# Attention of the second block by pairs of heads, with probabilities normalised before the transposes and output by features

## The chip, the cores and the metric

The kernel runs on one core of a Trainium2 chip. The metric is the device time of one execution in microseconds. A core has a matrix engine (PE, TensorE), VectorE (DVE), ScalarE (ACT), GpSimd (POOL) and SyncE (SP). Each works through its own list of instructions in order and waits for the others on counting signals (semaphores).

## What is computed

Two blocks in fp32, each of two layers, follow one another over 256 tokens of width 1024. The change lies in the second block, whose layers hold an FFN, a mixer and an FFN. In the mixer are two attentions (branch a, with a bias table over a neighbourhood, and branch b, with a window of 128 and a sink), each of six heads of 64, and a convolution:

```
def second_block(...):
    for l in range(DEPTH):
        ...
        ya = neighborhood_attention(qa, ka, va, ka_c, va_c, na_rpb[l], rows)
        yb = window_attention(qb, kb, vb, kb_c, vb_c, sw_sink[l])
        yc = conformer_conv(ux, conv_dw_w[l], conv_dw_b[l], conv_ln_g[l], conv_ln_b[l])
        x = x + mx[5] * merge_branches(ya, yb, yc, gx, b_gate[l], w_out_a[l], w_out_b[l], w_out_c[l], w_out[l])
        if not last:
            ya_c = context_attention(qa_c, ka_c, va_c, None)
            yb_c = context_attention(qb_c, kb_c, vb_c, sw_sink[l])
```

Queries are cut in tiles of 128. Tiles 0 and 1 are the tokens, which look at 256 own and 256 context keys (512); tiles 2 and 3 are the context, which looks at its own 256 keys and is there in layer 0 only. Branch b has two heads of keys and values for six heads of queries.

## The kernel before

**Order.** `plan()` writes one list of names for all engines: D is half a step of dense matmul, V an eviction, H and S the high and the low part of a weight (a cast on ACT and a subtraction on DVE), B a step of the second block's attention, C a tap of the convolution on DVE (two instructions), P a rotation, N a norm. Each engine has a generator for each name, and the list says in which order its parts stand on every engine. In the mixer the steps B are spread evenly between D, C and P by `mix()`: eight D with half of the first branch's, eight D with the rest and four C, then a stretch without D (B, four P and nine C), and then 24 D with all of the second branch's and 18 C. A D over 512 tokens is 12 matmuls of 512 columns, or nine or six in the products with the attention's output.

**Dense work.** Each weight is split in a high and a low fp32r part and each product takes three matmuls (`dense()`). Dense results go to the banks PS0 to PS2, and PS3 where four tiles are needed.

**Attention (`attention2` of the tensor, scalar and vector programs).** A job is a head of one query tile. In step i PE does the scores of job i (in PS4 or PS5 by turns), the transposes of the probabilities of job i - 1 (in PS6) and the product of job i - 2 with the values (in PS7). DVE adds the bias or the mask, takes the negated maximum, in branch b limits it by the sink, and then does the reciprocal of the sum of job i - 1 and scales the output of job i - 2 into O2. ACT does the exponential with its sum, in branch b the sink's too, and copies the transposed probabilities to PT2. After six heads, three transposes turn a tile of O2 into features, and ACT and DVE split it into YH2 and YL2. PE's transposes wait for the exponential alone:

```
                            q.wait_ge(*ab.at("exp", l, g))
                            if g:
                                q.wait_ge(*ab.at("pt", l, g - 1))
                            for x in range(2 if jobs[j][1] >= 2 else 4):
                                y = e.transpose(PS[6][:, 128 * x:128 * x + 128], P2[:, g % NB, 128 * x:128 * x + 128], IDN)
```

The wait for ACT's exponential of job i - 1 is met long before, since a D lies between two steps nearly everywhere.

Of the kernel before, what the change touches and what calls it, by code (L numbers as in the profile page):

```python
# [3 lines left out]
DEPTH = 2  # L4
# [50 lines left out]
def plan():  # L55
# [106 lines left out]
    def mixer(l, last, norm):  # L162
# [19 lines left out]
        nb = 6 * nq // 128 + 2  # L182
# [120 lines left out]
def program(nc, t, out):  # L303
# [81 lines left out]
    P2 = at("P2", 112.5, [128, 2, 512])  # L385
    PT2 = at("PT2", 116.5, [128, 2, 512])
    O2 = at("O2", 120.5, [128, 2, 384])
    ST2 = at("ST2", 123.5, [128, 256])
    TM2 = at("TM2", 124.5, [128, 3, 512])
# [58 lines left out]
    def jobs2(l):  # L448

        nt = 2 if l == DEPTH - 1 else 4  # L450
        return [[(br, q, h) for q in range(nt) for h in range(6)] for br in range(2)]


    def tensor_program(e):
# [17 lines left out]
        def operand(un, k, halves):  # L472
# [21 lines left out]
            if un.buf == "Y2":  # L494
                nt = 2 if l == DEPTH - 1 else 4
                if kk < 6:
                    q.wait_ge(*vb.at("y", l, kk // 3, nt - 1))
# [235 lines left out]
        def attention2():  # L733
            LAG, NB = 1, 2
            for l in range(DEPTH):
                nt = 2 if l == DEPTH - 1 else 4
                for br, jobs in enumerate(jobs2(l)):
                    n = len(jobs)
                    g0 = br * n
                    for i in range(n + 2 * LAG):  # L740
                        if i < n:
                            _, x, h = jobs[i]
                            g = g0 + i
                            if g < 2:
                                q.wait_ge(*vn.at("h", 4 + 3 * l, 7, 0))
                            else:
                                q.wait_ge(*ab.at("exp", l, g - 2))
                            k0, nk = (256, 256) if x >= 2 else (0, 512)
                            if br == 0:
                                hs, Q_, K_ = h % 2, QA[:, h // 2, :], QA[:, 3 + h // 2, :]  # L750
                                q.wait_ge(*ad.at("qa", l, h // 2))
                                q.wait_ge(*ad.at("qa", l, 3 + h // 2))
                            else:
                                hs, Q_, K_ = h // 3, QB[:, h % 3, :], QB[:, 3, :]
                                q.wait_ge(*vp.at("ro", l, h % 3))
                                q.wait_ge(*vp.at("ro", l, 3))
                            mm(PS[4 + g % 2][:, 0:nk], half(Q_, hs)[:, 128 * x:128 * x + 128],
                               half(K_, hs)[:, k0:k0 + nk]).then_inc(*pb.inc("s", l, g))
                        j = i - LAG
                        if 0 <= j < n:  # L760
                            g = g0 + j
                            q.wait_ge(*ab.at("exp", l, g))
                            if g:
                                q.wait_ge(*ab.at("pt", l, g - 1))
                            for x in range(2 if jobs[j][1] >= 2 else 4):
                                y = e.transpose(PS[6][:, 128 * x:128 * x + 128], P2[:, g % NB, 128 * x:128 * x + 128], IDN)  # L766
                            y.then_inc(*pb.inc("t", l, g))
                        j = i - 2 * LAG
                        if 0 <= j < n:
                            _, x, h = jobs[j]  # L770
                            g = g0 + j
                            vcol = 64 * h if br == 0 else 384 + 64 * (h // 3)
                            P = PS[7][:, 64 * (g % 4):64 * (g % 4) + 64]
                            q.wait_ge(*ab.at("pt", l, g))
                            if g:
                                q.wait_ge(*vb.at("o", l, g - 1))
                            k0, kt = (2, 2) if x >= 2 else (0, 4)
# [3 lines left out]
                            z.then_inc(*pb.inc("v", l, g))  # L781
                            if h == 5:
                                q.wait_ge(*vb.at("o", l, g))
                                if br or x:
                                    q.wait_ge(*vb.at("y", l, *((br, x - 1) if x else (0, nt - 1))))
                                else:
                                    q.wait_ge(*ad.at("v2", l, 3))
                                for y in range(3):
                                    z = e.transpose(PS[3][:, 128 * y:128 * y + 128],
                                                    O2[:, (nt * br + x) % 2, 128 * y:128 * y + 128], IDN)  # L790
                                z.then_inc(*pb.inc("y", l, br, x))
                        yield
# [11 lines left out]
        def lnorm():  # L804
            for l in range(DEPTH):
                nt = 2 if l == DEPTH - 1 else 4
                for x in range(nt):
                    P = PS[4]
                    q.wait_ge(*ab.at("exp", l, 12 * nt - 1))
# [22 lines left out]
    def scalar_program(e):  # L832
# [232 lines left out]
        def attention2():  # L1065
            LAG, NB = 1, 2
            for l in range(DEPTH):
                nt = 2 if l == DEPTH - 1 else 4
                for br, jobs in enumerate(jobs2(l)):
                    n = len(jobs)  # L1070
                    g0 = br * n
                    for i in range(n + 2 * LAG):
                        if i < n:
                            _, x, h = jobs[i]
                            g = g0 + i
                            nk = 256 if x >= 2 else 512
                            q.wait_ge(*vb.at("m", l, g))
                            if g >= NB:
                                q.wait_ge(*pb.at("t", l, g - NB))
                            af(P2[:, g % NB, 0:nk], PS[4 + g % 2][:, 0:nk], ACT.Exp, bias=ST2[:, g:g + 1],  # L1080
                               acc=ST2[:, 64 + g:65 + g]).then_inc(*ab.inc("exp", l, g))
                            if br:
                                af(ST2[:, 192 + i:193 + i], vec("sink", 6 * l + h), ACT.Exp, bias=ST2[:, g:g + 1]).then_inc(
                                    *ab.inc("sink", l, g))
                        j = i - LAG
                        if 0 <= j < n:
                            g = g0 + j
                            nk = 256 if jobs[j][1] >= 2 else 512
                            q.wait_ge(*pb.at("t", l, g))
                            if g >= NB:  # L1090
                                q.wait_ge(*pb.at("v", l, g - NB))
                            af(PT2[:, g % NB, 0:nk], PS[6][:, 0:nk], ACT.Copy).then_inc(*ab.inc("pt", l, g))
                        j = i - 2 * LAG
                        if 0 <= j < n and jobs[j][2] == 5:
                            x = jobs[j][1]
                            q.wait_ge(*pb.at("y", l, br, x))
                            af(YH2[:, 3 * br:3 * br + 3, 128 * x:128 * x + 128],
                               PS[3][:, 0:384].rearrange("p (i n) -> p i n", n=128), ACT.Copy).then_inc(*ab.inc("yh", l, br, x))
                        yield
# [27 lines left out]
    def vector_program(e):  # L1127
# [402 lines left out]
        def attention2():  # L1530
            LAG = 1
            for l in range(DEPTH):
                nt = 2 if l == DEPTH - 1 else 4
                for br, jobs in enumerate(jobs2(l)):
                    n = len(jobs)
                    g0 = br * n
                    for i in range(n + 2 * LAG):
                        if i < n:
                            _, x, h = jobs[i]
                            g = g0 + i  # L1540
                            nk = 256 if x >= 2 else 512
                            P, M = PS[4 + g % 2], ST2[:, g:g + 1]
                            q.wait_ge(*pb.at("s", l, g))
                            if x < 2 and br == 0:
                                q.wait_ge(*vk.at("bm", l))
                                tt(P[:, 0:256], P[:, 0:256], BM[:, x, h, :], ALU.add).then_inc(*vb.inc("b", l, g))
                                q.wait_ge(*vb.at("b", l, g))
                            elif x < 2:
# [424 lines left out]
```

## Time and profile before

| what | us |
|---|---|
| median of three runs | 2559.02 (2554.39 to 2559.24) |
| the profiled execution | 2551.03 |
| its span | 2549.2 |
| PE matmul busy | 2409.1 (95%) |
| DVE busy | 1576.8 (62%) |
| ACT busy | 874.9 (34%) |
| mean granted TensorE clock | 0.967 of full |

The profiled execution is 8 us below the median of the three timed runs, so differences are formed against its own 2551.03 and then put on the median. Busy shares are unions of instruction times. PE's instructions are pipelined, so what a matmul costs is read from one start to the next, not from its duration. An fp32 matmul stands in the trace as two instructions.

### The profile page before, as it was taken

How to read it: one execution, taken by the hardware profiler on the slowest of the kernel's cores; microseconds unless marked ns; L12 is line 12 of the kernel's file. 1: busy time of each engine (PE TensorE's matmuls, PEld its weight loads, DVE VectorE, ACT ScalarE, POOL GpSimd, SP SyncE). 2: the span in 40 equal slices, each digit the busy share in tenths (PEclk: the TensorE clock that was granted, in tenths of full speed). 3: DMA queues.
4: the chain of work that ended last, by engine and by line, in shares of the span. 5: the costliest groups of instructions: out<-in, count | busy, mean ns of one | idle time of the engine just before them, and what ended most of it. 6: DMA issues, size and time to landing. Idle time of an engine off the chain costs nothing.

```text
span 2549.2 us, 33154 instructions
## 1 busy us (share of the span) xinstructions
PE 2409.1 (95%) x13210; PEld 2028.7 (80%) x13210; DVE 1576.8 (62%) x2950; ACT 874.9 (34%) x1488; POOL 238.4 (9%) x321
## 2 busy tenths in 40 slices
PE   4898897899999999999999999999999999999998
PEld 4788776788888866678888888888888887788998
DVE  4886886576766446664469976654343345766655
ACT  3344344322222333433332222232222233444443
POOL 1010011100001200002211111100000030012001
PEclk9998998899999997999999999999999999999999
DMA  6543542254453310112336665522322232144553
GB/s 234 178 142 117 171 157 78 101 184 161 166 173 124 116 48 23 46 61 93 105 116 216 220 215 198 190 81 93 99 91 93 98 116 79 58 133 158 185 183 125
DMA packets 95354, 333.00 MB, mean 131 GB/s; under 512 B 11040, under 2 KB 13216, under 8 KB 94816
## 3 DMA queue, kind: packets, MB, share of 16 engines
q1 hardware_dynamic: 70496, 244.41, 28.7%
q0 software_dynamic: 23376, 84.80, 10.4%
q8 instruction: 105, 1.72, 0.3%
q10 hardware_dynamic: 1328, 1.66, 0.2%
q14 instruction: 49, 0.40, 0.1%
HBM read 329.78 MB, written 2.48 MB: 130 GB/s over the span
## 4 chain that ended last, share of the span: by engine, by line
PE 83%; DVE 10%; issue 3%; ACT 3%; POOL 1%; DMA 1%; ACTq 0%; POOLq 0%; DVEq 0%
PE PS L458 81%; DVE WL L1131 2%; PE PS L766 1%; ACT WH L840 1%; DVE NT L1140 1%; DVE HL L1140 1%; DVE JK L1141 1%; DVE AR L1141 1%; DVE PJ L1140 1%; DVE ST L1144 0%; DMA CST<-in_cst 0%; DVE CV L1140 0%; POOL SS L1722 0%; ACT HH L840 0%; DVE O L1135 0%
## 5 line engine op out<-in xcount | busy, mean ns | idle before, releaser
L840 ACT ACTIVATE WH<-RAW 128x1024 fp32r<-128x1024 f32 (+2 forms) x482 | 494.4, 1026 | 1061.1 <-PE PS L458 1060.8
L458 PE MATMUL PS<-HH,WH 128*128 128x512 f32 (+1 forms) x2136 | 763.7, 358 | 13.2 <-DVE HL L1140 5.9
L458 PE MATMUL PS<-HH,WL 128*128 128x512 f32 (+1 forms) x2136 | 751.7, 352 | 0.0
L458 PE MATMUL PS<-HL,WH 128*128 128x512 f32 (+1 forms) x2136 | 751.5, 352 | 0.0
L1131 DVE TENSOR_TENSOR WL<-RAW,WH 128x1024 fp32r<-128x1024 f32 (+2 forms) x482 | 572.1, 1187 | 171.7 <-ACT WH L840 170.6
L458 PEld LDWEIGHTS PS<-HH,WH 128*128 128x128 f32 x2136 | 407.9, 191 | 81.4 <-issue 9.2
L458 PEld LDWEIGHTS PS<-HH,WL 128*128 128x128 f32 x2136 | 408.0, 191 | 57.5
L458 PEld LDWEIGHTS PS<-HL,WH 128*128 128x128 f32 x2136 | 408.7, 191 | 55.6
L458 PE MATMUL PS<-GH,WH 128*128 128x512 f32 (+1 forms) x776 | 271.0, 349 | 0.0
L458 PE MATMUL PS<-GH,WL 128*128 128x512 f32 (+1 forms) x776 | 270.2, 348 | 0.0
L458 PE MATMUL PS<-GL,WH 128*128 128x512 f32 (+1 forms) x776 | 270.2, 348 | 0.0
L1140 DVE SCALAR_TENSOR_TENSOR FT<-FT,PS 128x512 f32<-128x512 f32 (+1 forms) x185 | 110.4, 597 | 252.0 <-ACT FT L840 184.0
L1141 DVE SCALAR_TENSOR_TENSOR AR<-AR,CB 128x1024 f32<-128x1024 f32 x144 | 178.0, 1236 | 2.4 <-DMA AR<-in_w_adaT 2.4
L1140 DVE SCALAR_TENSOR_TENSOR X<-PS,MOD,X 128x256 f32<-128x256 f32 x192 | 86.5, 480 | 140.5 <-PE PS L458 140.2
L458 PEld LDWEIGHTS PS<-GH,WH 128*128 128x128 f32 x776 | 146.0, 188 | 21.0 <-DVE GL L1131 0.2
L458 PEld LDWEIGHTS PS<-GL,WH 128*128 128x128 f32 x776 | 146.0, 188 | 20.7
L458 PEld LDWEIGHTS PS<-GH,WL 128*128 128x128 f32 x776 | 146.0, 188 | 20.6
L1801 POOL DMA_DIRECT2D AR<-in_w_adaT x144 | 77.0, 535 | 811.9 <-DVE AR L1141 691.6
L841 ACT ACTIVATE P<-PS,ST 128x512 f32<-128x512 f32 (+2 forms) x104 | 57.9, 557 | 235.2 <-DVE ST L1144 142.6
L1141 DVE SCALAR_TENSOR_TENSOR JK<-AR,CB 128x1024 bf16<-128x1024 f32 x112 | 137.5, 1228 | 1.4 <-DMA AR<-in_w_adaT 1.4
L458 PE MATMUL PS<-H1H,WH 128*128 128x256 f32 x384 | 117.6, 306 | 16.6 <-DVE WL L1131 15.0
L1722 POOL TENSOR_TENSOR SS<-SS,SQ 128x256 f32<-128x256 f32 (+1 forms) x59 | 65.9, 1117 | 706.0 <-ACT SQ L840 703.7
(219 smaller groups left out, 3045.5 us busy)
## 6 DMA issues: line engine op xcount, KB each, us to landing
RAW<-in_wst SPq DMA_DIRECT2D x420, 512.0 KB, 3.5
AR<-in_w_adaT POOLq DMA_DIRECT2D x144, 512.0 KB, 3.8
RAW<-in_wst SPq DMA_DIRECT2D x48, 384.0 KB, 3.0
BM<-rpb_rows POOLq DMA_DIRECT2D x48, 64.0 KB, 2.9
CB<-in_cc POOLq DMA_DIRECT2D x2, 1024.0 KB, 9.2
RAW<-in_wst SPq DMA_DIRECT2D x8, 256.0 KB, 2.7
RAW<-in_wst SPq DMA_DIRECT2D x4, 396.0 KB, 5.2
rpb_rows<-in_rpb POOLq DMA_DIRECT2D x2, 697.5 KB, 9.9
```

What stands on the lines that cost most here:

```text
L458: return e.matmul(o, l, r, start=start, stop=stop)
L766: y = e.transpose(PS[6][:, 128 * x:128 * x + 128], P2[:, g % NB, 128 * x:128 * x + 128], IDN)
L840: return e.activation(o, i, f, bias=bias, scale=scale)
L841: return e.activation(o, i, f, bias=bias, scale=scale, accum_out=acc)
L1131: return e.tensor_tensor(out=o, in0=a, in1=b, op=op)
L1140: return e.scalar_tensor_tensor(out=o, in0=a, scalar=s, in1=b, op0=op0, op1=op1)
L1141: return e.scalar_tensor_tensor(out=o, in0=a, scalar=s, in1=b, op0=op0, op1=op1, accum_out=acc)
L1722: return e.tensor_tensor(out=o, in0=a, in1=b, op=op)
L1801: e.dma_start(AR[:, y % 2, :], t["w_adaT"][l, x, :, :]).then_inc(adw[y % 2], 16)
```

## The change

A job becomes a pair of heads of one query tile: heads 2p and 2p + 1 in branch a, p and p + 3 in branch b, which lie in partitions 0 to 63 and 64 to 127 of one tile of Q and K. There are half as many jobs and `nb` follows: 14 steps for 26 in layer 0, eight for 14 in layer 1. In step i:

- PE does both scores, one in each row half of the array, in PS4 and PS5, with one signal; then the transposes of both heads of job i - 1 in PS6 and PS7, now after a wait for DVE's normalisation ("n"); and, at odd query tiles only, one product for two tiles of queries with the values stationary (64 columns) and the probabilities moving (256 columns), the two heads in the two column halves of PS3. The output is then by features, and O2 with its transposes is gone.
- DVE does two adds, two maxima (and two limits), then one reciprocal for both sums of job i - 1 and two multiplications of the probabilities P2 in place. The scaling of the output is gone. YL2 is taken for a pair of heads and two query tiles.
- ACT does two exponentials, two copies to PT2 and, at odd tiles, one copy to YH2.
- The scores of a job wait for the second exponential of the job before (PS4 and PS5 are used by each job).
- Some buffers are moved and enlarged, and the rows of `w_out_b_2` are put in the order of the pairs on the host.

```diff
-        nb = 6 * nq // 128 + 2
+        nb = 3 * nq // 128 + 2
...
-    P2 = at("P2", 112.5, [128, 2, 512])
-    PT2 = at("PT2", 116.5, [128, 2, 512])
-    O2 = at("O2", 120.5, [128, 2, 384])
+    P2 = at("P2", 112.5, [128, 4, 512])
+    PT2 = at("PT2", 120.5, [128, 2, 4, 256])
...
-        return [[(br, q, h) for q in range(nt) for h in range(6)] for br in range(2)]
+        return [(p, x) for p in range(3) for x in range(2 if l == DEPTH - 1 else 4)]
+
+    def keys2(x):
+
+        return (2, 2) if x >= 2 else (0, 4)
...
+                            if i or br:
+                                q.wait_ge(*ab.at("exp", l, *((br, i - 1, 1) if i else (0, n - 1, 1))))
...
+                            k0, kt = keys2(x)
+                            for a in range(2):
+                                z = mm(PS[4 + a][:, 0:128 * kt], half(Q_, a)[:, 128 * x:128 * x + 128],
+                                       half(K_, a)[:, 128 * k0:128 * (k0 + kt)])
+                            z.then_inc(*pb.inc("s", l, br, i))
+                        j = i - 1
+                        if 0 <= j < n:
+                            for a in range(2):
+                                q.wait_ge(*vb.at("n", l, br, j, a))
+                                if j or br:
+                                    q.wait_ge(*ab.at("pt", l, *((br, j - 1, a) if j else (0, n - 1, a))))
+                                for y in range(keys2(jobs[j][1])[1]):
+                                    z = e.transpose(PS[6 + a][:, 128 * y:128 * y + 128],
+                                                    P2[:, 2 * (j % 2) + a, 128 * y:128 * y + 128], IDN)
+                                z.then_inc(*pb.inc("t", l, br, j, a))
+                        j = i - 2
+                        if 0 <= j < n and jobs[j][1] % 2:
...
-                                z = mm(P, PT2[:, g % NB, 128 * y:128 * y + 128], V2[:, k0 + y, vcol:vcol + 64], y == 0, y == kt - 1)
...
+                                for a in range(2):
+                                    q.wait_ge(*ab.at("pt", l, br, j, a))
+                                    c = 128 * p + 64 * a if br == 0 else 384 + 64 * a
+                                    z = mm(PS[3][64 * a:64 * a + 64, 0:256], V2[:, k0 + y, c:c + 64], PT2[:, a, y, :], y == 0,
+                                           y == kt - 1)
+                            z.then_inc(*pb.inc("v", l, br, j))
...
-                                z.then_inc(*pb.inc("y", l, br, x))
...
+                            q.wait_ge(*pb.at("s", l, br, i))
...
+                            for a in range(2):
+                                P, g = PS[4 + a], 2 * (n * br + i) + a
+                                M = ST2[:, g:g + 1]
+                                if x < 2:
+                                    q.wait_ge(*vb.at("b", l, br, i, a))
+                                rmax(M, P[:, 0:nk], True).then_inc(*vb.inc("m" if br == 0 else "m0", l, br, i, a))
...
+                            e.reciprocal(Y, Z).then_inc(*vb.inc("r", l, br, j))
+                            q.wait_ge(*vb.at("r", l, br, j))
+                            nk = 128 * keys2(jobs[j][1])[1]
+                            for a in range(2):
+                                P = P2[:, 2 * (j % 2) + a, 0:nk]
+                                ts(P, P, Y[:, a:a + 1], None, ALU.mult, None).then_inc(*vb.inc("n", l, br, j, a))
+                        j = i - 2
+                        if 0 <= j < n and jobs[j][1] % 2:
+                            p, x = jobs[j]
+                            c = slice(128 * (x - 1), 128 * (x + 1))
+                            q.wait_ge(*ab.at("yh", l, br, j))
+                            tt(YL2[:, 3 * br + p, c], PS[3][:, 0:256], YH2[:, 3 * br + p, c].bitcast(f32),
+                               ALU.subtract).then_inc(*vb.inc("y", l, br, j))
```

On PE, one step of branch a in layer 0 between two halves of dense steps reads as follows in the kernel before (CST holds the identity; s_att2_act and s_att2_dve are the attention's signals from ACT and from DVE):

```order
L458 MATMUL PS2<-HH_49,WL 128x512
L458 MATMUL PS4<-QA_90 128x512
L766 MATMUL PS6<-CST,P2_98 128x128 [waits s_att2_act]
L766 MATMUL PS6<-CST,P2_98 128x128 x3
L458 MATMUL PS7<-V2_93,PT2_99 128x64 x3
L458 MATMUL PS7<-V2_93,PT2_99 128x64 [waits s_dense_act]
L458 MATMUL PS2<-HH_49,WH 128x512
```

and in the changed one, at a step with 256 keys that holds a product with the values too:

```order
L460 MATMUL PS2<-HH_49,WL 128x512
L460 MATMUL PS4<-QA_90 128x256 [waits s_att2_act]
L460 MATMUL PS5<-QA_90 128x256
L767 MATMUL PS6<-CST,P2_98 128x128 [waits s_att2_act,s_att2_dve]
L767 MATMUL PS6<-CST,P2_98 128x128
L767 MATMUL PS7<-CST,P2_98 128x128 [waits s_att2_act,s_att2_dve]
L767 MATMUL PS7<-CST,P2_98 128x128
L460 MATMUL PS3<-PT2_99,V2_93 64x256 x8
L460 MATMUL PS2<-HH_49,WH 128x512
```

Two scores stand together, the transposes have gained a wait for DVE, and the dense matmul of PS2 stands behind all of them.

On DVE, the third step of branch a in layer 0 before the change (BM is the bias table, ST2 holds maxima, sums and reciprocals):

```order
L1131 TENSOR_TENSOR PS4<-PS4,BM_91 128x256 [waits s_att2_pe]
L1144 TENSOR_REDUCE ST2_101<-PS4 128x1 [waits s_att2_dve]
L1566 RECIPROCAL ST2_101<-ST2_101 128x1 [waits s_att2_act]
L1135 TENSOR_SCALAR O2_100<-PS7,ST2_101 128x64 [waits s_att2_pe]
```

and the second step after it:

```order
L1128 TENSOR_TENSOR PS4<-PS4,BM_91 128x256 [waits s_att2_pe]
L1128 TENSOR_TENSOR PS5<-PS5,BM_91 128x256
L1141 TENSOR_REDUCE ST2_100<-PS4 128x1 [waits s_att2_dve]
L1141 TENSOR_REDUCE ST2_100<-PS5 128x1 [waits s_att2_dve]
L1566 RECIPROCAL ST2_100<-ST2_100 128x2 [waits s_att2_act]
L1132 TENSOR_SCALAR P2_98<-P2_98,ST2_100 128x512 [waits s_att2_dve]
L1132 TENSOR_SCALAR P2_98<-P2_98,ST2_100 128x512
```

The multiplications of P2 by the reciprocals, for which PE's transposes of the job before wait, stand behind the adds and maxima of this step, and these behind PE's scores of this step.

## Rows read from the trace of the kernel before

**Rows 1.** The page: engine totals; the chain that ended last

```profile
PE 2409.1 (95%) x13210; PEld 2028.7 (80%) x13210; DVE 1576.8 (62%) x2950; ACT 874.9 (34%) x1488; POOL 238.4 (9%) x321
PE 83%; DVE 10%; issue 3%; ACT 3%; POOL 1%; DMA 1%; ACTq 0%; POOLq 0%; DVEq 0%
```

**Rows 2.** Timeline, PE, a step with 512 keys (start, us, what)

```profile
914.24 0.48 PE L458 MATMUL PS<-HH,WH 128*128 128x512 f32 x1
...
920.02 1.12 PE L458 MATMUL PS<-QA 64*128 64x512 f32 x2
921.07 0.66 PE L766 MATMUL PS<-CST,P 128*128 128x128 f32 x4
921.56 1.00 PE L458 MATMUL PS<-V,PT 128*128 128x64 f32 x8
922.37 0.47 PE L458 MATMUL PS<-HH,WH 128*128 128x512 f32 x1
...
925.34 1.12 PE L458 MATMUL PS<-QA 64*128 64x512 f32 x2
```

**Rows 3.** Timeline, PE, a step with 256 keys

```profile
1121.55 0.70 PE L458 MATMUL PS<-QB 64*128 64x256 f32 x2
1122.18 0.44 PE L766 MATMUL PS<-CST,P 128*128 128x128 f32 x2
1122.45 0.56 PE L458 MATMUL PS<-V,PT 128*128 128x64 f32 x4
1122.82 0.48 PE L458 MATMUL PS<-YH,WH 128*128 128x512 f32 x1
```

**Rows 4.** Timeline, PE, transposes of O2 behind a product with values

```profile
945.67 1.00 PE L458 MATMUL PS<-V,PT 128*128 128x64 f32 x8
947.05 0.55 PE L789 MATMUL PS<-CST,O 128*128 128x128 f32 x3 [0.38 <-DVE O L1135]
947.35 0.48 PE L458 MATMUL PS<-HH,WH 128*128 128x512 f32 x1
```

**Rows 5.** Timeline, DVE, one step of branch a in layer 1

```profile
2163.95 0.43 DVE L1131 TENSOR_TENSOR PS<-PS,BM 128x256 f32<-128x256 f32 x1
2164.41 0.69 DVE L1144 TENSOR_REDUCE ST<-PS 128x1 f32<-128x512 f32 x1
2165.02 0.15 DVE L1566 RECIPROCAL ST<-ST 128x1 f32<-128x1 f32 x1
```

**Rows 6.** Groups by form, DVE: xcount, busy us, mean ns

```profile
L1144 DVE TENSOR_REDUCE ST<-PS 128x1 f32<-128x256 f32 x40 | 16.9, 423 | 17.8 <-PE PS L458 17.3
L1135 DVE TENSOR_SCALAR ST<-ST,SM 128x1 f32<-128x1 f32 x36 | 7.7, 214 | 1.3
L1136 DVE TENSOR_SCALAR TM<-TM 128x512 f32<-128x512 f32 x2 | 0.9, 428 | 5.3 <-ACT TM L840 5.3
L1136 DVE TENSOR_SCALAR CV<-HP,VEC 128x512 f32<-128x512 f32 x2 | 1.0, 542 | 0.0
```

**Rows 7.** Timeline, PE, eight instructions in the two column halves (first block)

```profile
116.03 0.45 PE L458 MATMUL PS<-VC,MK 128*64 128x65 f32 x8
116.41 0.39 PE L458 MATMUL PS<-H1H,WH 128*128 128x256 f32 x1
```

**Rows 8.** PE behind a gap: timeline, and a window (PE busy, granted clock, DMA)

```profile
898.87 0.50 PE L458 MATMUL PS<-HH,WH 128*128 128x512 f32 x1 [2.18 <-ACT V L840]
...
900.00:902.00 2.00, 2.00 (x7) 0.50 0.00 0
```

**Rows 9.** Timeline, PE, ends of the stretches without dense work, layers 0, 1

```profile
976.54 0.70 PE L458 MATMUL PS<-QA 64*128 64x256 f32 x2
1014.18 2.07 PE L458 MATMUL PS<-QB 64*128 64x512 f32 x2
...
2157.53 1.12 PE L458 MATMUL PS<-QA 64*128 64x512 f32 x2
2183.27 0.56 PE L458 MATMUL PS<-HH,WH 128*128 128x256 f32 x1
```

More of the change, by code:

```diff
@@ L733, in attention2 @@
         def attention2():
-            LAG, NB = 1, 2
             for l in range(DEPTH):
[L736 to L740, printed above, removed]
+                jobs = jobs2(l)
+                n = len(jobs)
+                for br in range(2):
+                    for i in range(n + 2):
                         if i < n:
-                            _, x, h = jobs[i]
-                            g = g0 + i
-                            if g < 2:
+                            p, x = jobs[i]
+                            if i or br:
+                                q.wait_ge(*ab.at("exp", l, *((br, i - 1, 1) if i else (0, n - 1, 1))))
+                            else:
@@ L757, in attention2 @@
[L757 to L767, printed above, removed]
@@ L781, in attention2 @@
[L781 to L790, printed above, removed]
-                                z.then_inc(*pb.inc("y", l, br, x))
+                                for a in range(2):
[3 more added lines that the diff above has]
+                                           y == kt - 1)
@@ L808, in lnorm @@
                     P = PS[4]
-                    q.wait_ge(*ab.at("exp", l, 12 * nt - 1))
+                    q.wait_ge(*ab.at("exp", l, 1, 3 * nt - 1, 1))
                     if x:
@@ new lines, in attention2 @@
+                jobs = jobs2(l)
+                n = len(jobs)
+                for br in range(2):
+                    for i in range(n + 2):
+                        if i < n:
+                            p, x = jobs[i]
+                            nk = 128 * keys2(x)[1]
+                            for a in range(2):
+                                g = 2 * (n * br + i) + a
+                                q.wait_ge(*vb.at("m", l, br, i, a))
+                                if i >= 2 or br:
+                                    q.wait_ge(*pb.at("t", l, *((br, i - 2, a) if i >= 2 else (0, n - 2 + i, a))))
+                                af(P2[:, 2 * (i % 2) + a, 0:nk], PS[4 + a][:, 0:nk], ACT.Exp, bias=ST2[:, g:g + 1],
+                                   acc=ST2[:, 64 + g:65 + g]).then_inc(*ab.inc("exp", l, br, i, a))
+                                if br:
+                                    y = 192 + 2 * i + a
+                                    af(ST2[:, y:y + 1], vec("sink", 6 * l + p + 3 * a), ACT.Exp, bias=ST2[:, g:g + 1]).then_inc(
+                                        *ab.inc("sink", l, i, a))
+                        j = i - 1
+                        if 0 <= j < n:
+                            x = jobs[j][1]
+                            kt = keys2(x)[1]
+                            c = slice(128 * (x % 2), 128 * (x % 2) + 128)
+                            for a in range(2):
+                                q.wait_ge(*pb.at("t", l, br, j, a))
+                                if x % 2 == 0 and (j or br):
+                                    q.wait_ge(*pb.at("v", l, *((br, j - 1) if j else (0, n - 1))))
+                                af(PT2[:, a, 0:kt, c], heads(PS[6 + a][:, 0:128 * kt], 128), ACT.Copy).then_inc(
+                                    *ab.inc("pt", l, br, j, a))
+                        j = i - 2
+                        if 0 <= j < n and jobs[j][1] % 2:
+                            p, x = jobs[j]
+                            q.wait_ge(*pb.at("v", l, br, j))
+                            c = slice(128 * (x - 1), 128 * (x + 1))
+                            af(YH2[:, 3 * br + p, c], PS[3][:, 0:256], ACT.Copy).then_inc(*ab.inc("yh", l, br, j))
```

149 lines of the change are left out of this document (48 added, 101 removed).

## Prediction

> **What bounds the kernel now.** I read the page first: PE is busy for 95% of the span and makes up 83% of the chain that ended last, against 10% for DVE [rows 1]. So what an edit adds to PE's list, and each wait that PE runs into, is paid nearly in full; work on DVE and ACT is free until PE waits for it. Then the timeline of the mixers. A step B of the attention stands alone between two blocks of dense matmuls. From one block to the next it reads 920.02, 921.07, 921.56 and 922.37 [rows 2]: 1.05 us of scores over 512 keys, 0.49 of transposes, 0.81 of products with the values, and no idle note anywhere. Two dense halves took 5.78 us (914.24 to 920.02) and one 2.97 (922.37 to 925.34), so a half is 2.81 and the interruption itself costs 0.16. A step is 2.51 us. With 256 keys it is 0.63 + 0.27 + 0.37 [rows 3] + 0.16 = 1.43. The three transposes of O2 put another 0.87 behind a product (945.67 + 0.81 to 947.35, 0.38 of it idle for DVE) [rows 4]. Last the two stretches without dense work: 37.6 us in layer 0 (976.54 to 1014.18) and 25.7 in layer 1 (2157.53 to 2183.27) [rows 9].
>
> **What PE saves between dense blocks.** Counted from the lists, 43 steps of 512 keys, 13 of 256 and nine groups of O2 transposes lie in the stretches with D: 43 x 2.51 + 13 x 1.43 + 9 x 0.87 = 134 us. After the change there are 20 pairs of 512 and nine of 256 keys.
>
> Scores: a pair costs at most two scores in a row. The slope between 512 and 256 keys is 0.42 us [rows 2, 3], so 512 keys are 0.84 of streaming and 0.21 of start; two in a row are 1.89 us, and 1.05 for 256 keys. At least it costs one score, 1.05 and 0.63. Each fp32 product is two instructions, and PE issues both of the first head, then both of the second; if halves can overlap at all, only the second of head 0 with the first of head 1 does. That leaves three quarters: 1.47 and 0.84. I take these: 20 x 1.47 + 9 x 0.84 = 37 (bounds 27 and 47).
>
> The trace has no two row halves back to back, but it has column halves: eight instructions of 65 columns, heads alternating between the halves, take 0.38 us in all (116.03 to 116.41) [rows 7]. At the streaming rate of the scores (0.42 us for two instructions of 256, so 0.0008 a column) the eight alone are 0.43 us with no start, so they must overlap. The page TensorEngine Tiling of the Trainium skill (Key Properties) says that different tiles can execute weight loads and matmuls in parallel; the column halves agree, and no row here shows row halves. By that rule taken in full the scores would be 27 us, 10 less.
>
> Values: a pair with 512 keys is now 16 instructions of 256 columns, 0.21 each: 3.4 us in a row, or nine slots of 0.21 = 1.9 if neighbours overlap; half for 256 keys. For eight and four of them: 19 us, or 34 in a row. I take 19, since rows 7 are just this form. Transposes are as many as before, in groups of eight (twice 0.49 less a start, 0.9) or four: 19 x 0.9 + 8 x 0.5 = 21. Interruptions: 29 x 0.16 = 5. Sum 82; saved 134 - 82 = 52 us, between 62 (all halves at once) and 27 (none).
>
> **What PE now waits for.** This is the term that decides. In step i PE does both scores and then the transposes of pair i - 1, which wait for "n", DVE's multiplication by the reciprocal. As the two lists show, DVE comes to "n" of pair i - 1 only behind the adds and maxima of pair i, and these wait for the scores that PE has just done. Between scores and transposes PE has nothing else in its list, and the next dense block stands behind them. So DVE's whole step lies on PE's path. From the rows: an add is followed by its dependent maximum after 0.46 us, a maximum over 512 by the next instruction after 0.61 [rows 5]; over 256 it is 0.42 long [rows 6], 0.34 to the next by the same overlap; the multiplication of 512 columns is bounded by 0.43 and 0.54 [rows 6], I take 0.5, and 0.3 for 256. For branch a and 512 keys: first add 0.35, second add to maximum 0.46, two maxima 1.22, reciprocal 0.18, multiplication 0.5 = 2.7 us; 2.5 if the pair before had 256 keys. With 256 keys there is no add: two maxima 0.68, reciprocal 0.18, multiplication 0.5 or 0.3, with handover 1.4 and 1.2. Branch b has shorter adds but two limits and the sum with the sink more, each near the reciprocal's 0.15 [rows 5]: 0.25 on top. Per step between dense blocks, behind a step i of at least 1: layer 0, branch a 2.7 + 1.4 + 1.2 + 2.5 + 2.7 + 1.4 = 12; branch b 25 over eleven steps; layer 1, three of 2.7 and five of 2.95 = 23. Together **60 us in 25 waits**, and about 0.1 at each second head, 3 us. Before, the same place waited for an exponential that was long done.
>
> On these sections alone the change costs 60 + 3 - 52 = **11 us**.
>
> **The clock.** Behind a gap of 2.18 us on PE the granted clock of the window from 900 was 0.50, the lower of the two levels, 1.2 GHz [rows 8]. All 2 us of that window ran at half rate, which loses 1 us. Sixteen of the new waits are 2.5 us or longer; with the dense blocks and the steps between them they are eight to ten us apart. At 1 us each they cost 16; if all PE work between two such waits ran low, about 4.5 each or 72; if the clock stayed up, 0. I take 1.4 each, **22 us**. The page TensorE: Matmul & The Clock Gate of the Trainium skill (HAM oscillation) warns of this: gaps between bursts of matmuls put the array back to its lower clock burst after burst. [...]
>
> **The stretches without D.** Layer 0 keeps six of its 14 steps here, four ropes and nine convolution taps. The new handover of YL2 adds a detour at odd query tiles: DVE waits for PE's product and ACT's copy before it goes on. Laid out by hand with the same prices it comes to 36 us at the full clock, with some 9 us of PE work on the path; the layer 1 stretch to 23.5 with 5. The stretches are 37.6 and 25.7 now [rows 9]. With the PE part at half clock they would be 45 and 28.5. Between -4 and +10, I take **+4**.
>
> **What costs nothing.** DVE does as much as before: the scaling of O is replaced by the multiplications, the reciprocals halve; at 62% busy it has room. ACT's copies to PT2 are the same columns. The scores of the next pair wait for the second exponential, which ends two exponentials after the second maximum; PE's own wait and a dense block (2.81 us a half, in layer 1 half of that) cover it; if that cover were gone, I estimate 1 us a step. Weights: casts and splits are held up for some 5 us a step by ACT's and DVE's waits, against two units of dense work in hand. If that were not enough, a wait for WL would show. DMA and SP don't change.
>
> **Sum.** 11 + 22 + 4 = +37 us on the profiled 2551.03; on the median of 2559.02 this is 2596. A difference under 0.2% (5 us) can't be told from no change.
>
> **The rivals.**
>
> *Waits as worked out, halves partly overlapping* (forecast): 2574 to 2622 by the clock's term between 0 and 48 us. Chance 0.62. For it: the two lists fix the order, and all prices but the overlap are durations of the same operations.
>
> *The halves don't overlap*: products run in a row. Saved 27 in place of 52, and some 6 more in the stretches without D: +31, 2627 (2605 to 2650). For it: no row shows row halves. Against it: rows 7. Chance 0.17, most of it for the scores alone, where it is +10.
>
> *No change*: all halves at once (10 us better) and a clock that stays up (22 better) leave +5 or less, 2559 to 2564. Against it: [rows 8]. Chance 0.08.
>
> *Faster*: the wait for "n" is shorter than worked out, since the adds and maxima of a pair, in two banks, follow each other faster than those of rows 5, which lie between other work. The point from which it decides: with the clock up the change breaks even at 49 / 25 = 2.0 us a wait, against 2.4 on average here. At 1.4 us a wait it gives 2559 - 15 = 2544, within 2530 and 2554. Against it: each price is an instruction's own time on DVE. Chance 0.09.
>
> *The change doesn't do what it says* (PE isn't held up since "n" comes early) falls under faster; only the last step of a branch, where DVE has no scores to wait for, has "n" early.
>
> *A starved dense block* (casts late) adds a few us in layer 1, where a half is only some 1.4 us: within the range, 0.04 by itself at about 2630.
>
> **How the numbers follow.** The likeliest case alone spans 2574 to 2622, and its middle is 2596. For eight in ten the range has to take in the upper rival's middle and the case of no change: 2560 to 2632. Slower by over 0.2%: 0.62 + 0.17 + 0.04 and a little of the case at the edge, 0.84; same 0.07; faster 0.09.
>
> **What the profile after will show.** (1) In the waits of PE, a row for the transposes' line released by DVE P (the multiplication), about 25 to 33 times and 55 to 75 us in all, longest about 3; if it holds under 35 us, the main step is wrong. (2) Pairs of scores at 1.4 to 1.5 us from start to start to the end; 1.9 says that row halves don't overlap, 1.05 that they do in full. (3) Products with stationary values at 1.9 us for 16 instructions. (4) The granted clock at 0.50 in several windows of the mixers between 900 and 1170 and again after 2110; the mean of the span falls from 0.967 by about 0.015. (5) PE's busy time lower, its idle time higher, and DVE's part of the chain above 10%. (6) The stretches without D within some 8 us of 37.6 and 25.7. The prediction is wrong if PE has something to do between the scores and the transposes that I don't see, or if a wait of 2.5 us leaves the clock up.

## The result and the profile after

The changed kernel takes 2605.22 us (median of four runs, 2603.76 to 2609.25) against 2559.13 of the kernel before: ratio 1.0187, 95% interval 1.0169 to 1.0204, 46 us slower. The profiled execution took 2609.25 us, 58 us more than that of the kernel before (2551.03). Its engine totals and the chain that ended last, to be held against [rows 1]:

```profile
PE 2384.9 (91%) x12934; PEld 2004.2 (77%) x12934; DVE 1576.0 (60%) x2902; ACT 875.2 (34%) x1494; POOL 236.8 (9%) x321
...
PE 81%; DVE 12%; issue 3%; ACT 3%; POOL 1%; DMA 1%; ACTq 0%; POOLq 0%; DVEq 0%
```

TensorE (PE) is busy for 24 us less, while the span is 58 us longer: PE does have less to do, and idle time more than ate it up. The waits of PE say which (line waited for: total, times, longest):

```profile
PE PS L767 <- DVE P L1132: 88.1, 34, 5.4
...
PE PS L767 <- ACT P L835: 5.4, 2, 2.7
```

Line 767 holds the row transposes of P, line 1132 is DVE's multiplication by the reciprocal. The second row is the same line waiting in branch b of layer 0, twice 2.7 us, where the profile names ACT; its neighbours with the same work are put down to DVE, so I count it with them. Together 93.5 us. The timeline of PE shows one such wait between dense blocks; the step of 256 keys follows, and further down are products with the values and two transposes of branch b:

```profile
918.22 0.40 PE L460 MATMUL PS<-HH,WL 128*128 128x512 f32 x1
918.55 1.13 PE L460 MATMUL PS<-QA 64*128 64x512 f32 x4
922.33 1.51 PE L767 MATMUL PS<-CST,P 128*128 128x128 f32 x8 [2.65 <-DVE P L1132]
923.49 0.77 PE L460 MATMUL PS<-HH,WH 128*128 128x512 f32 x1
924.06 0.63 PE L460 MATMUL PS<-HL,WH 128*128 128x512 f32 x1
...
933.30 0.70 PE L460 MATMUL PS<-QA 64*128 64x256 f32 x4
935.46 1.10 PE L767 MATMUL PS<-CST,P 128*128 128x128 f32 x8 [1.45 <-DVE P L1132]
...
982.76 0.70 PE L460 MATMUL PS<-QA 64*128 64x256 f32 x4
...
985.41 1.95 PE L460 MATMUL PS<-PT,V 128*64 128x256 f32 x16
987.29 0.70 PE L460 MATMUL PS<-QB,CST 128*128 128x256 f32 x2
...
1026.23 0.79 PE L460 MATMUL PS<-HH,WH 128*128 128x512 f32 x1
...
1041.11 1.09 PE L767 MATMUL PS<-CST,P 128*128 128x128 f32 x8 [2.83 <-DVE P L1132]
1049.08 1.93 PE L767 MATMUL PS<-CST,P 128*128 128x128 f32 x8 [1.90 <-DVE P L1132]
```

Three things are to be read here. The four instructions of a pair of scores take 1.13 us, as the two of one head did [rows 2]. Then PE stands still for 2.65 us. Behind that, the dense matmuls take 0.63 us each, where those ahead took 0.40: the lower clock (the granted clock of 924 to 926 us is 0.50). The last two rows are the same eight transposes at either level, 1.09 and 1.93 us. The timelines of DVE and ACT fill the gap:

```profile
919.73 0.76 DVE L1128 TENSOR_TENSOR PS<-PS,BM 128x256 f32<-128x256 f32 x2 [4.28 <-PE PS L460]
920.40 1.28 DVE L1141 TENSOR_REDUCE ST<-PS 128x1 f32<-128x512 f32 x2
921.11 0.69 ACT L835 ACTIVATE P<-PS,ST 128x512 f32<-128x512 f32 x1 [6.44 <-DVE ST L1141]
921.59 0.15 DVE L1566 RECIPROCAL ST<-ST 128x2 f32<-128x2 f32 x1
921.78 0.88 DVE L1132 TENSOR_SCALAR P<-P,ST 128x512 f32<-128x512 f32 x2
```

DVE idled for 4.28 us, although the reciprocal's input had been there long since: the exponentials of the pair before were done when ACT fell idle, 6.44 us before 921.11, that is by 914.67. DVE stood in its list at the next pair's scores. The mean clock of the span (view of the cores) went from 0.967 to 0.951:

```profile
core 0: 2607.5 us, clock 0.951
```

Since the clock has two levels, 1.0 and 0.5, time at the lower one is twice (1 - mean) times the span: 168 us before, 255 us now. All such figures below are worked out so, from the profiled executions; the mean is given to 0.001, so each is good to some 3 us.

### The profile page after: what moved, and what is told of

It reads as the page before. It is cut to its first block, busy times and chain, and to the rows that moved or that the text cites. A ratio compares the mean times of both kernels' runs of the same rounds, so it can differ in the third digit from the quotient of the medians.

```text
span 2607.5 us, 32546 instructions
## 1 busy us (share of the span) xinstructions
PE 2384.9 (91%) x12934; PEld 2004.2 (77%) x12934; DVE 1576.0 (60%) x2902; ACT 875.2 (34%) x1494; POOL 236.8 (9%) x321
## 4 chain that ended last, share of the span: by engine, by line
PE 81%; DVE 12%; issue 3%; ACT 3%; POOL 1%; DMA 1%; ACTq 0%; POOLq 0%; DVEq 0%
PE PS L460 79%; DVE WL L1128 2%; PE PS L767 2%; DVE ST L1141 2%; ACT WH L834 1%; DVE NT L1137 1%; DVE HL L1137 1%; DVE CV L1137 1%; DVE JK L1138 1%; DVE AR L1138 1%; DVE P L1132 1%; DVE PJ L1137 0%; DVE PS L1128 0%; DMA CST<-in_cst 0%; POOL SS L1717 0%
## 5 line engine op out<-in xcount | busy, mean ns | idle before, releaser
L460 PEld LDWEIGHTS PS<-HH,WH 128*128 128x128 f32 x2136 | 413.9, 194 | 88.2 <-issue 12.8
L460 PEld LDWEIGHTS PS<-HH,WL 128*128 128x128 f32 x2136 | 413.5, 194 | 58.2
L460 PEld LDWEIGHTS PS<-HL,WH 128*128 128x128 f32 x2136 | 414.4, 194 | 57.0
L767 PE MATMUL PS<-CST,P 128*128 128x128 f32 x240 | 46.0, 347 | 93.4 <-DVE P L1132 88.1
```

Of the source, the lines that this page charges most:

```text
L460: return e.matmul(o, l, r, start=start, stop=stop)
L767: z = e.transpose(PS[6 + a][:, 128 * y:128 * y + 128], P2[:, 2 * (j % 2) + a, 128 * y:128 * y + 128], IDN)
```

## Experiments

Six kernels take the change apart and three go on from the best of them. Each ratio is against the kernel before, run in the same session. Its median lay between 2556.6 and 2559.1 us from session to session, so differences in microseconds between kernels of different sessions are good to some 3 us.

**1. Normalisation first** (below: the first kernel). Only DVE's order is changed.

```diff
                     for i in range(n + 2):
+                        j = i - 1
+                        if 0 <= j < n:
...
+                            e.reciprocal(Y, Z).then_inc(*vb.inc("r", l, br, j))
...
+                                ts(P, P, Y[:, a:a + 1], None, ALU.mult, None).then_inc(*vb.inc("n", l, br, j, a))
                         if i < n:
...
                             q.wait_ge(*pb.at("s", l, br, i))
...
-                            e.reciprocal(Y, Z).then_inc(*vb.inc("r", l, br, j))
...
-                                ts(P, P, Y[:, a:a + 1], None, ALU.mult, None).then_inc(*vb.inc("n", l, br, j, a))
```

> The changed kernel with one thing moved: on DVE, the reciprocal and the normalisation of the pair before are ahead of the wait for the scores, the adds and the maxima of this pair, no longer behind them. Everything is still computed. Theory A (the loss is TensorE's wait for the normalised probabilities, because DVE takes them in order behind the next pair's adds and maxima; these gaps also lower the clock, and the odd tiles' subtraction makes the stretches without dense work longer): the 88.1 us of waits of the row transposes for P fall below 30, of which most are left in the two stretches without dense work; the half-clock time falls by some 60 to 90 us, worth about 20; time 2500 to 2535 us, faster than both kernels. Theory B (the loss is in the work that TensorE got: changes between half rows, whole rows and half columns, or in the clock for another reason): the waits turn into others of the same length or go without the time falling by as much; time 2580 us or more.

Measured: 2520.48 us, ratio 0.9853 (0.9833 to 0.9873), 85 us under the changed kernel and faster than the kernel before. PE's waits and the cores' view:

```profile
PE PS L767 <- DVE P L1132: 40.4, 21, 5.4
```

```profile
core 0: 2520.6 us, clock 0.965
```

Waits for P fell from 88.1 to 40.4 us, not below 30; between 900 and 960 us none is left. Of what remains, 12.7 and 6.7 us lie in the two stretches without dense work, and 12.8 us between the dense blocks of branch b in layer 1. Time at the lower clock fell from 255 to 176 us, as forecast. PE's idle time fell by 48 us (222.6 to 174.8), as much as its waits for P: theory B is out, since nothing else took their place.

**2. Normalisation between the adds and the maxima**, a half dose: DVE's step is adds of pair i, reciprocal and multiplications of pair i - 1, maxima of pair i.

> The changed kernel with the normalisation of the pair before put between the adds and the maxima of this pair: the wait for P then stands behind 0.76 us of adds and no longer behind 2.04 us of adds and maxima. Everything is still computed. If the time follows the wait (theory A), the waits in steps of 512 keys fall from 2.6 and 1.45 us to about 1.4 and 0.2, the total of 93 us to 50 to 60, and the time lies between the two orders, 2545 to 2570 us. If the clock falls with any gap, however short, it stays above 2580; if only long gaps count, it comes near the kernel with the normalisation first, 2520 to 2540.

Measured: 2547.59 us, ratio 0.9962 (0.9948 to 0.9975). The wait of the same step on PE's timeline fell from 2.65 to 1.45, and that behind 256 keys, 1.45 in the changed kernel, to 0.79:

```profile
920.84 1.10 PE L767 MATMUL PS<-CST,P 128*128 128x128 f32 x8 [1.45 <-DVE P L1132]
...
931.72 1.09 PE L767 MATMUL PS<-CST,P 128*128 128x128 f32 x8 [0.79 <-DVE P L1132]
```

All its waits for P are 61.5 us, just over the 50 to 60 expected, and the clock's mean is 0.965, as with the normalisation first. The windows of 80 us in the middle of branch b in layer 0, between dense blocks, give PE's busy time, that of the other engines and the granted clock; first this kernel, with waits of 0.55 to 1.39 us in it, then the changed kernel, with 1.76 to 2.83:

```profile
1030.00:1110.00 80.00, 68.84 (x351) 47.76 (x352) 55.55 (x136) 36.57 (x101) 0.00 (x0) 1.00 0.16 55
```

```profile
1030.00:1110.00 80.00, 64.32 (x278) 43.74 (x276) 42.92 (x102) 29.24 (x77) 0.00 (x0) 0.89 0.13 43
```

With the shorter waits the clock stayed at its upper level, with the longer ones it didn't. What is left to the full cure, 27 us, is mostly the waits' own length (21 us). The time came out as the first outcome on record, the clock as the third.

**3. The wait kept and filled.** Extra matmuls stand in the gap, so the clock is priced apart from the wait.

```diff
+                                if a == 0 and i < n:
+                                    for _ in range(16 if jobs[i][1] < 2 else 8):
+                                        mm(PS[6][:, 0:256], HH[:, 0, 0:128], HH[:, 0, 0:256])
                                 q.wait_ge(*vb.at("n", l, br, j, a))
```

> The changed kernel with the wait kept and filled: ahead of the wait for the normalised probabilities TensorE does 16 (step with a pair of 512 keys) or 8 (256 keys) extra matmuls of 128 x 256 into the bank that the transposes then overwrite; the output is as before. It prices the clock apart from the wait. If the gaps are what lowers the clock: the half-clock time falls from 260 us towards 170 and the time falls by 20 to 28 us, to about 2577 to 2585 us. If the clock fell for another reason, or its price is small: 2600 us or more (the extra work, some 1.7 us at full clock, is longer than the shorter waits).

Measured: 2565.45 us, ratio 1.0033 (1.002 to 1.0045): 40 us faster than the changed kernel, with 416 instructions more. Its timeline, its groups (busy us, mean ns) and its clock:

```profile
918.28 1.13 PE L460 MATMUL PS<-QA 64*128 64x512 f32 x4
919.34 2.17 PE L460 MATMUL PS<-HH 128*128 128x256 f32 x16
922.05 1.09 PE L770 MATMUL PS<-CST,P 128*128 128x128 f32 x8 [0.55 <-DVE P L1135]
```

```profile
L460 PE MATMUL PS<-HH 128*128 128x256 f32 x416 | 59.6, 295 | 0.0
```

```profile
core 0: 2567.3 us, clock 0.970
```

The extra work is busy for 59.6 us; PE's idle time fell by 53 (222.6 to 169.2), so the filling itself is nearly neutral. The rest of PE's work shrank from 2384.9 to 2398.1 - 59.6 = 2338.5 us, 46 us, for 101 us less at the lower clock: 0.46 us of work a microsecond. The price is above what I expected, by nearly a factor of two. The same kernel measures the work that the change saves: 2338.5 against 2409.1 [rows 1] is 71 us, of which some 6 are the 14 us less that it spends at the lower clock than the kernel before; at an equal clock it is **about 65 us**.

**4. The scores apart.** The first kernel (experiment 1), with the second head's scores behind the transposes, so that the row halves can't overlap.

```diff
-                            for a in range(2):
-                                z = mm(PS[4 + a][:, 0:128 * kt], half(Q_, a)[:, 128 * x:128 * x + 128],
-                                       half(K_, a)[:, 128 * k0:128 * (k0 + kt)])
-                            z.then_inc(*pb.inc("s", l, br, i))
+                            def score(a):
+                                return mm(PS[4 + a][:, 0:128 * kt], half(Q_, a)[:, 128 * x:128 * x + 128],
+                                          half(K_, a)[:, 128 * k0:128 * (k0 + kt)])
+                            score(0)
...
                                 z.then_inc(*pb.inc("t", l, br, j, a))
+                        if i < n:
+                            score(1).then_inc(*pb.inc("s", l, br, i))
```

> The first of these kernels (normalisation ahead) with the second head's scores put behind the transposes of the pair before, so that the two row halves are not used one straight after the other. Everything is still computed. If the pair's four instructions in 1.13 us mean that the two halves work at the same time, each head alone takes its 1.1 us (512 keys) or 0.7 us (256 keys): 24 x 1.1 + 12 x 0.7 = 35 us more on TensorE than the first, and the time rises by 20 to 40 us over it. If the time of 1.13 us is only what the records show (ends are modelled), or a head alone takes half of it, the time rises by less than 8 us.

Measured: 2583.66 us, ratio 1.0098 (1.0074 to 1.0121), 63 us over the first kernel.

```profile
918.65 1.12 PE L460 MATMUL PS<-QA 64*128 64x512 f32 x2
919.70 1.09 PE L768 MATMUL PS<-CST,P 128*128 128x128 f32 x8
920.73 1.12 PE L460 MATMUL PS<-QA 64*128 64x512 f32 x2
921.78 0.50 PE L460 MATMUL PS<-HH,WH 128*128 128x512 f32 x1
```

Each head alone takes from 918.65 to 919.70 and from 920.73 to 921.78, 1.05 us twice; together they take 1.06. The four groups of scores rose from 37.2 to 77.5 us, 40 in all. Over 256 keys a pair takes 0.63 us in the first kernel (934.79 to 935.42), as one head alone does [rows 3]. So it isn't a fixed cost that a pair shares: twice the 0.84 us of streaming would not fit in 1.06. The halves do work at the same time, and the records don't mislead. Beyond my 20 to 40 us lies time at the lower clock, 233 us against 176, which at 0.46 is another 26; part of it is in the 40 already.

**5. The subtraction later.** DVE takes the low half of the output (YL2), which waits for ACT's copy of the products, at the start of the next step.

```diff
                     for i in range(n + 2):
+                        if i >= 3 and jobs[i - 3][1] % 2:
+                            low_y(i - 3)
...
-                        j = i - 2
-                        if 0 <= j < n and jobs[j][1] % 2:
-                            p, x = jobs[j]
-                            c = slice(128 * (x - 1), 128 * (x + 1))
-                            q.wait_ge(*ab.at("yh", l, br, j))
-                            tt(YL2[:, 3 * br + p, c], PS[3][:, 0:256], YH2[:, 3 * br + p, c].bitcast(f32),
-                               ALU.subtract).then_inc(*vb.inc("y", l, br, j))
+                        if i == n + 1:
+                            low_y(n - 1)
```

Here `low_y(j)` holds the removed lines from `p, x` on.

On top of the first kernel:

> The first of these kernels with the subtraction that makes the low half of the attention output (DVE, at the odd tiles, behind ACT's conversion of the products just made) moved a step later, to the start of the next step. Everything is still computed. Theory A: DVE no longer stands before ACT's conversion (33 waits, 87 us in the changed kernel), the stretches without dense work become 3 to 7 us shorter each, and the time is 5 to 15 us below the first. Rival: with the normalisation ahead, the detour is beside other work or the next products wait for the later subtraction; within 4 us of the first.

Measured: 2503.65 us, ratio 0.9792 (0.9772 to 0.9812), 17 us under the first. DVE's waits of YL for ACT fell from 58.4 to 22.0 us, PE's for P from 40.4 to 31.0; the stretch in layer 0 went from 38.8 to 35.9 us and that in layer 1 from 21.7 to 20.3, together 4 us and less than the 3 to 7 each that I expected; time at the lower clock fell from 176 to 155 us. The same edit alone, in the changed kernel:

> The changed kernel with only the later subtraction (it stands at the start of the next step on DVE), the normalisation being left behind the next pair's adds and maxima. Behind the moved normalisation the same edit was worth 17 us. If that was the odd tiles' detour in itself, it is worth about as much here: 2583 to 2595 us. If it paid only because the normalisation came first (here the subtraction, now ahead of the adds and maxima, is paid for by them and by the wait for P), the time is within 6 us of 2605.

Measured: 2586.75 us, ratio 1.0112 (1.0089 to 1.0135), 18 us under the changed kernel. PE's waits for P are 80.7 us, the stretches 39.9 and 26.6 (4 us less), time at the lower clock 228 us (27 less, 12 us by experiment 3). DVE's waits of YL for ACT, in the kernel before, in the changed kernel and in the one with both edits (with this edit alone they are 31.7 us):

```profile
DVE YL L1131 <- ACT YH L840: 23.3, 28, 1.5
...
DVE YL L1128 <- ACT YH L834: 87.1, 33, 6.7
...
DVE YL L1128 <- ACT YH L834: 22.0, 24, 4.9
```

The detour cost 17 to 18 us with either order: the two faults of DVE's list add up (85 and 18 apart, 102 together). In the kernel with both edits, the best, the step reads:

```profile
917.39 1.13 PE L460 MATMUL PS<-QA 64*128 64x512 f32 x4
918.45 1.10 PE L767 MATMUL PS<-CST,P 128*128 128x128 f32 x8
919.30 0.48 PE L460 MATMUL PS<-HH,WH 128*128 128x512 f32 x1
```

with no wait: 1.91 us for the scores and transposes of two heads, where one head's took 1.54 (920.02 to 921.56, [rows 2]).

**6. The products by head**, on the best kernel: all of one column half, then all of the other. With it, in the same session, the best kernel again, and that kernel with its remaining gaps filled.

```diff
-                            for y in range(kt):
-                                q.wait_ge(*ad.at("v2", l, k0 + y))
-                                for a in range(2):
+                            for a in range(2):
+                                for y in range(kt):
+                                    q.wait_ge(*ad.at("v2", l, k0 + y))
```

> The best kernel so far (normalisation ahead, subtraction a step later) with the products with the values in another order: all of one head's (columns 0 to 63 of the array) and then all of the other's (columns 64 to 127), in place of one head and the other in turn. Everything is still computed. If the two column halves work at the same time, as the row halves do (16 instructions of 128 x 256 in 1.95 us, 0.12 each), the order takes that away: the 33.7 us of this group rise to 55 to 65 and the time rises by 15 to 35 us over the best. If the column halves only follow each other at 0.12 us an instruction, the time stays within 5 us of the best.

> The best kernel so far again, in the same session as the two others, so that they can be compared with it: 2501 to 2509 us.

> The best kernel so far with 12 extra matmuls of 128 x 256 ahead of the wait for P in the steps that lie in the two stretches without dense work (first branch, from the ninth pair on in layer 0, from the fourth on in layer 1); the output is as before. If these gaps still lower the clock (20 us of half-clock time from 985 to 1013 us, 0.45 us lost for each): 3 to 9 us below the best. If the extra work delays the steps, whose next scores wait for ACT's exponentials and not for this: within 3 us, or slower.

Measured: 2519.54, 2508.56 and 2504.89 us, ratios 0.9854 (0.9841 to 0.9868), 0.9815 (0.98 to 0.9829) and 0.9801 (0.9787 to 0.9816). The 16 products by head, and their group:

```profile
937.06 2.86 PE L460 MATMUL PS<-PT,V 128*64 128x256 f32 x16
```

```profile
L460 PE MATMUL PS<-PT,V 128*64 128x256 f32 x240 | 46.0, 423 | 0.0
```

and in the best kernel in turn:

```profile
938.81 1.95 PE L460 MATMUL PS<-PT,V 128*64 128x256 f32 x16
```

```profile
L460 PE MATMUL PS<-PT,V 128*64 128x256 f32 x240 | 34.9, 436 | 0.0
```

By head they take 11.1 us more, where I expected 20 to 30, and the time rises by 11 us, less than the 15 to 35 on record. The 16 take 2.79 us by head (937.06 to 939.85), 0.17 an instruction, and 1.88 in turn, 0.12; the granted clock is 1.00 in both. So the column halves overlap in part: in full it would be 1.4. Filling the last gaps brought time at the lower clock from 166 to 125 us, but put in 16.5 us of work; 4 us less with intervals that overlap is no difference. The best kernel itself lies 5 us above its first run (2503.65), in another session.

Its remaining waits for P are 29.4 us in 18: 15.6 in seven in the two stretches, and 13.8 between dense blocks, mostly in branch b of layer 1. There DVE stands at another wait ahead of the normalisation, that of a weight's low part for ACT's cast: 2.10 us before 2190.97, while the reciprocal follows at 2192.30 and PE waits 1.84 us up to 2193.04. I have no kernel without it.

## Why the prediction was right

The forecast was 2596, within 2560 to 2632, slower with 0.84; 2605 is the likeliest case, 9 us beside its middle. The mechanism was right: DVE's order puts its whole step on PE's path. Its terms, in the profiled executions:

**What PE now waits for: right, in mechanism and size.** 60 + 3 us in 25 waits were forecast for the sections between dense blocks. Of the 93.5 us, 17.3 lie in the stretch without D of layer 0 and 11.4 in that of layer 1, which leaves 64.8 in 27. The single ones for branch a in layer 0 are 2.65 and 1.45 (forecast 2.7 and 1.4). Experiment 1 takes 44 of the 65 us away by one exchange in DVE's list, and experiment 2, the half dose, 26. Point (1) was too low in all, 55 to 75 us in 25 to 33 waits for 93.5 in 36, since it left most of those in the stretches (28.7 us) out; and the longest, 5.4, is in such a stretch, not about 3.

**What PE saves between dense blocks: mis-sized, 52 for about 62.** "If halves can overlap at all, only the second of head 0 with the first of head 1 does. That leaves three quarters: 1.47 and 0.84" is the step that failed. Pairs take 1.06 and 0.63, one score each, which is the lower bound of the working: 20 x 1.06 + 9 x 0.63 = 27 in place of 37. The products came as forecast, 1.88 to 1.95 for 16. The rule of the Trainium skill (TensorEngine Tiling, Key Properties), which the prediction weighed and didn't follow, gave 27 us for the scores, and the row halves agree with it in full; the column halves do in part only (experiment 6). Experiment 4 shows that the overlap is real.

**The clock: mis-sized, 22 for about 40.** 255 - 168 = 87 us more at the lower level, at the 0.46 of experiment 3, is 40 us. "Sixteen of the new waits are 2.5 us or longer" counted too few, and "I take 1.4 each" was too low. In the 4 us behind each wait between dense blocks the granted clock was 0.50 to 0.65 at 21 of the 27: at 16 of the 17 of 2.5 us and more, and at five of the six of 1.76 to 1.90, which the forecast took to be free; behind the four of 1.45 and less it was 1.00. That makes 40 / 21 = 1.9 us a gap, and one agrees: behind the wait at 922.33 the matmuls were still slow at 925.77 (0.63). That the clock stayed up behind one wait of 2.83 (1081.03) says that the length of a wait alone doesn't decide. With the dose of experiment 2 the clock stayed as it is without the waits. So of what the gaps cost, their own length (65 us) is some three fifths and their echo on the clock (40 us) two fifths.

**The stretches without D: +7 for +4.** They are 43.5 us (982.76 to 1026.23) and 27.2, from 37.6 and 25.7 [rows 9]. The detour of YL2 is there, as DVE's waits for ACT show (87.1 us in 33, against 23.3 in 28 before), and experiment 5 takes 17 to 18 us back by removing it. Only about 4 of them lie in these stretches; the others are waits and clock elsewhere, where the prediction gave the detour nothing: that is the term it left out. In branch b of layer 1, for one, three of the changed kernel's six waits are 3.4 to 3.7 us for 2.95 forecast; with the subtraction alone moved one is left above 2.83.

The terms as measured: 65 - 62 + 40 + 7 = 50, for 58 between the two profiled executions; part of the 40 is inside the 7, so 8 us or more are unaccounted for. Between the medians it is 46, since the profiled execution of the kernel before was 8 us faster than its median: its clock was 0.967, and its executions in the later sessions had 0.960 to 0.966. The forecast put +37, formed against that fast execution, on the median, where it came out 9 us low; against the execution it was formed on it would have been 21 low. And the two errors of sizes, 10 us too little saved and 18 too little lost to the clock, had opposite signs and partly cancelled. So the sign and the range are earned, but that the middle is hit within 9 us is luck.

**Rivals.** Halves that don't overlap is refuted (experiment 4). No change needed full overlap and a clock that stays up: the first came true for the row halves, the second not; experiment 3, which has both but pays for the filling, comes out 0.3% slower. Faster needed waits under 2.0 us with the clock up: experiment 2, with 1.7 a wait over all its waits (61.5 in 36), is 0.4% faster, as that break-even says; it left the prediction's own +4 of the stretches out, and with it would be 45 / 25 = 1.8.

## What to carry to other kernels

When two stages of a pipeline share an in-order engine, put what an earlier job needs to finish ahead of what a later job needs to start, and never ahead of it a wait for work that the bounding engine has just been given: here one exchange in DVE's list turned +1.9% into -1.5%, and moving one subtraction made it -2.1% (-1.9% when run again). The change itself was good, worth about 65 us of TensorE's work; its order hid that. Put matmuls in different halves of the array directly behind each other, and where there are many in the column halves, let the halves alternate (11 us here).

## What the runs showed of the hardware

- Two row halves overlap in full, even with both instructions of one fp32 product ahead of both of the other: 1.06 us for two heads, 1.05 for one.
- Column halves overlap in part: 16 instructions of 256 columns took 1.88 us in turn and 2.79 one half after the other.
- With waits of 1.76 to 2.83 us between dense blocks the granted clock of 1030 to 1110 us was 0.89, with 0.55 to 1.39 us in their place 1.00. Waits of 1.76 to 1.90 us were followed by the lower clock at five of six places. Time at the lower clock cost 0.46 us of work per microsecond, and filling the gaps with matmuls that nobody needs won 40 us.
